# First unit of a latent projection: products ordered by high and low parts, input scales on ScalarE's DMA queue, the sum of squares half a unit later

## The chip, the cores and the metric

The kernel runs on one core of a Trainium2 chip. The metric is the device time of one execution in microseconds; the time before is the median of three runs. Engines are named as the profile names them: PE is TensorE, DVE is VectorE, ACT is ScalarE, POOL is GpSimd, SP is SyncE. DMAs are issued here from SP and, in a few places, from ACT.

## The reference

Two transformer-like blocks run one after the other on 512 tokens of width 1024. Only the beginning of the first matters for this change:

```
u = x * rsqrt(mean(x*x) + EPS) * g_mix_pre
z = u @ w_in[0]
... q_lat, kv_lat, k_rope are columns of z ...
q = rmsnorm(q_lat) * g_q_lat @ w_q_up
k_pe = rope(k_rope, positions)
```

Behind it follow latent attention, a gated convolution, a mixing layer, a feed-forward layer, gated linear attention and an indexed sparse attention. They are computed as before.

## The kernel before, in words

All matrices are kept in f32 and every product is made of three matmuls on rounded parts. A weight block `w` becomes `w_hi` (rounded) and `w_lo` (what is left), an operand becomes `op_hi` and `op_lo`; `split_mm` (lines 747 to 753) issues hi x hi, hi x low operand and low weight x hi into one PSUM bank. The sequence on every engine is written out by hand, and engines meet at counting semaphores. `Steps` names each step of a stage (`hi3`, `lo3`, `acc7`, `sum`), and `at("acc7")` is the count to wait for.

Weights come in **units** of 512 KB, eight blocks of 128 x 128. SP loads a unit into one of four `raw` buffers. POOL splits it: line 723 writes `w_hi` and raises `hi_ready`, line 725 writes `w_lo` and raises `split_ready`. There are two split slots, so POOL may begin unit u only when PE has finished unit u-2 (`unit_done`).

The first four units, 0 to 3, hold w_in for four output tiles, two of the eight contraction blocks k in each (`blockwise`): unit 0 has k = 0 and 1, unit 1 has 2 and 3, unit 2 has 4 and 5, unit 3 has 6 and 7. Banks 0 to 3 take all of them, so each unit is 24 matmuls. Units 4 and 5 hold one further output tile each.

In stage `start` the input x arrives transposed in `h`, in eight tiles of 128 x 512. For each tile m:

- ACT (line 1683) writes `op_hi[m]` = rounded h[m] times its gain column, step `hi{m}`; it then squares h[m] (line 1686), step `sq{m}`;
- DVE writes `op_lo[m]` (line 2408), step `lo{m}`, and adds the square to a running sum (line 2405), step `acc{m}`.

The gain columns (`gain`, 289 per partition) arrive by one DMA. The norm of x is not applied to the operand; the sum of squares is taken over partitions by one matmul with ones, `full_sum(4)` (line 769), step `sum`. ACT takes the root (line 1649), DVE the reciprocal (`rs`, line 2484), and the projected tiles are multiplied by `rs` when they leave PSUM (`z0`, `z1`, ...: line 2402). Between `rs` and `z0` DVE's list also holds the rotary angles, in this order: `pos` (line 2487), `ang0` (2451), `turn` (2454), `whole` (2456), `red1` to `red3` (2408), `clip` (2461). Then come `z0`, `z1`, `z2`, and `acc1`, `acc2`, the sum of squares of the query latent. PE, in stage `lat`, does six of the eight blocks of unit 4 (18 matmuls), waits for `acc2`, does `sum_q` (line 775), the last two blocks, `root_q` (line 789), and goes on to unit 5. That is the only way into the rest of the program.

PE's order before is units 0 and 1, then `sum`, then units 2 and 3.

Of the kernel before, what the change touches and what calls it, by code (L numbers as in the profile page):

```python
# [50 lines left out]
U0 = {}  # L51
# [156 lines left out]
def build(nc, ins, out):  # L208
    ctx = ExitStack()
    with ctx:  # L210
# [7 lines left out]
        w_hi = sb("w_hi", [P, SLOTS, 8, P], F32R)  # L218
        w_lo = sb("w_lo", [P, SLOTS, 8, P], F32R)
        op_hi = sb("op_hi", [P, KD, T], F32R)  # L220
        op_lo = sb("op_lo", [P, KD, T], F32R)
# [10 lines left out]
        gain = sb("gain", [P, GAINS], F32)  # L232
        st = sb("st", [P, 64], F32)
        ps = [ctx.enter_context(nc.psum_tensor(f"bank{b}", [P, T], F32)) for b in range(8)]
# [109 lines left out]
        hi_ready = sem("hi_ready")  # L344
        half_hi, half_ready = sem("half_hi"), sem("half_ready")
        split_ready = sem("split_ready")
        unit_done = sem("unit_done")
        gain_in, p_in, pos_in = sem("gain_in"), sem("p_in"), sem("pos_in")
        x_in = [sem(f"x_in{n}") for n in range(KD // 2)]
        x_first = sem("x_first")  # L350
        cst_in, out_sem = sem("cst_in"), sem("out_sem")
# [206 lines left out]
        def enter(eng, who, name, others=("act", "dve", "pe"), after=None, drained=True):  # L558


            k = ORDER.index(name)
            if k:
                before = S[after or ORDER[k - 1]][who]
                eng.wait_ge(before.sem, before.total)
            if who == "pe":
                used = U0[name] if name in U0 else 0
                if used and drained:
                    eng.wait_ge(unit_done, used)
            mine = S[name][who]
            eng.sem_inc(mine.sem, mine.credit)  # L570
            for other in others:
                if other != who:
                    eng.wait_ge(S[name][other].sem, S[name][other].credit)
            return S[name]["act"], S[name]["dve"], S[name]["pe"]
# [5 lines left out]
        def _(sp):  # L580
# [37 lines left out]
            n = LOADS  # L618
            load_from(0, 0)
            sp.dma_start(h[:, 0], ins["x"][0]).then_inc(x_first, 16)  # L620
            sp.dma_start(gain[:, :], ins["gains"]).then_inc(gain_in, 16)
            sp.dma_start(h[:, 1], ins["x"][1]).then_inc(x_in[0], 16)
            load_from(1, 1)
            for k in range(1, KD // 2):
# [123 lines left out]
        def _(pe):  # L748
# [18 lines left out]
            def full_sum(bank, x=acc):  # L767

                return pe.matmul(ps[bank][:, :], ones, x, start=True, stop=True)
# [22 lines left out]
            def blockwise(u0, before, units=range(4)):  # L792

                d = S[before]["dve"]
                for c in units:
                    pe.wait_ge(split_ready, u0 + c + 1)
                    for kk in range(2):
                        k = 2 * c + kk
                        pe.wait_ge(d.sem, d.at(f"lo{k}"))
                        for m in range(4):  # L800
                            mm = split_mm(ps[m][:, :], w_hi[:, (u0 + c) % 2, 4 * kk + m], w_lo[:, (u0 + c) % 2, 4 * kk + m],
                                          op_hi[:, k], op_lo[:, k], k == 0, k == KD - 1)
                    mm.then_inc(unit_done, 1)

            a, d, z = enter(pe, "pe", "start")
            blockwise(U0["lat"], "start", range(2))
            pe.wait_ge(cst_in, 16)
            pe.wait_ge(d.sem, d.at("acc7"))
            z.done(full_sum(4), "sum")
            blockwise(U0["lat"], "start", range(2, 4))  # L810

            a, d, z = enter(pe, "pe", "lat", ())
            u = U0["lat"]
# [17 lines left out]
            a, d, z = enter(pe, "pe", "attn", ())  # L831
# [88 lines left out]
            for k in range(2):  # L920
                u = attn_unit(f"V{k}")
                pe.wait_ge(split_ready, u + 1)
                wh, wl = [w[:, u % 2, 0:4].rearrange("p k n -> p (k n)") for w in (w_hi, w_lo)]
                for t in range(QT):
                    mm = split_mm(ps[3 + t][:, :], kvn_hi[:, k, t * P:(t + 1) * P], kvn_lo[:, k, t * P:(t + 1) * P], wh, wl, k == 0, k == 1)
                mm.then_inc(unit_done, 1)
            for p in range(NH // 2):
                x, y = 2 * p, 2 * p + 1
# [41 lines left out]
            a, d, z = enter(pe, "pe", "mix", ())  # L970
# [17 lines left out]
            u = U0["mix"]  # L988
# [12 lines left out]
            a, d, z = enter(pe, "pe", "wo", ())  # L1001
            for m in range(KD):
                u = U0["wo"] + m
# [22 lines left out]
            a, d, z = enter(pe, "pe", "res1", (), drained=False)  # L1026
# [13 lines left out]
            u = U0["up0"]  # L1040
            for c in range(4):
                s = (u + c) % 2
                pe.wait_ge(split_ready, u + c + 1)
                for kk in range(2):
                    k = 2 * c + kk
# [7 lines left out]
                    for m in range(4):  # L1053
                        mm = pe.matmul(ps[m][:, :], w_hi[:, s, 4 * kk + m], op_lo[:, k], start=False, stop=k == KD - 1)
# [6 lines left out]
            for n, x in enumerate((acc, fx[:, 11, :])):  # L1061
# [4 lines left out]
                for t in range(QT):  # L1066
                    mm = pe.matmul(ps[5][:, t:t + 1], x[:, t * P:(t + 1) * P], ones[:, 0:1], start=n == 0 and t == 0, stop=n == 1,
                                   skip_group_check=True)
# [6 lines left out]
            for half in (0, 1):  # L1075
                name = f"up{half}"
                a, d, z = enter(pe, "pe", name, () if half == 0 else ("act", "dve", "pe"))
                u = U0[name]
# [24 lines left out]
                a, d, z = enter(pe, "pe", name, ())  # L1103
                if half == 0:
                    with pe.Fori(0, 2) as i:
                        for m2 in range(2):
# [3 lines left out]
                            for v in range(3):  # L1110
                                c = 3 * m2 + v
                                pe.wait_ge(split_ready, i * 6 + (U0[name] + c + 1))
                                for kb in range(8):
# [3 lines left out]
                                    m, k = n // HJ, n % HJ  # L1117
# [8 lines left out]
                else:  # L1126
                    for g in range(KD // 2):
# [3 lines left out]
                        for v in range(3):  # L1131
                            u = U0[name] + 3 * g + v
                            pe.wait_ge(split_ready, u + 1)
                            for kb in range(min(8, 2 * HJ - 8 * v)):
                                m, k = divmod(8 * v + kb, HJ)
# [507 lines left out]
        def _(act):  # L1643
# [23 lines left out]
            def proj_out(name, m, bank):  # L1667
# [5 lines left out]
                    act.wait_ge(unit_done, U0[name] + 1)  # L1673
                hi(a, f"e{m}", ebuf[:, m, :], ps[bank][:, :])

            act.wait_ge(cleared, 1)
            act.activation(st[:, 62:63], st[:, 63:64], ACT.Sqrt, bias=st[:, 63:64])
            act.wait_ge(gain_in, 16)
# [1913 lines left out]
```

## Time and profile before

| | |
|---|---|
| time, median of 3 runs | 1747.75 us (1746.61 to 1748.42) |
| the profiled execution's own time | 1746.92 us |
| its span, first to last instruction | 1745.1 us |
| mean granted TensorE clock | 0.996 |
| PE busy | 98% of the span |
| DVE, ACT, POOL busy | 59%, 36%, 57% |

The span lies inside the execution's own time, 1.8 us of which are outside it. The chain that ended last is 87% PE over the whole program; the busy share of PE says little of the first 60 us, in which other engines feed it, and those are what the change touches. Times in the text are microseconds from the span's start unless a whole time is meant.

### The profile page before, as it was taken

Reading aid. Unit: us, or ns where it says so; the run is one execution under the profiler, and the core shown is the slowest. Engines: PE = TensorE matmul, PEld = TensorE weight load, DVE = VectorE, ACT = ScalarE, POOL = GpSimd, SP = SyncE. Lnnn points to the kernel's source line nnn. Section 1 sums busy time; section 2 is a strip of 40 time slices with the busy share of each in tenths; the row PEclk is TensorE's granted clock in tenths of the full one; section 3 lists DMA queues with packets and bytes.
Section 4 is the critical chain, followed back from the end, with each engine's and each line's share of the span. In section 5 each row is a group of like instructions: output and inputs, shape, how many; then the busy total and the mean of one; then the engine's idle time right before and its main releaser. Section 6 shows DMA issues by size and latency. Waiting matters only on the chain.

```text
span 1745.1 us, 22351 instructions
## 1 busy us (share of the span) xinstructions
PE 1709.6 (98%) x7966; PEld 1418.3 (81%) x7966; DVE 1023.3 (59%) x1680; ACT 629.4 (36%) x1182; POOL 986.5 (57%) x586
## 2 busy tenths in 40 slices
PE   7999999999999999998999999999999999999998
PEld 6788788788877888887788888888878888888887
DVE  6778543345651554254778745646757977776244
ACT  4455311243312222043734332332433127766022
POOL 5655466666666666664664556555565663333654
PEclk9999999999999999998999999999999999999999
DMA  5222222222223222322222222222232221111222
GB/s 205 91 76 86 81 97 96 97 94 88 97 97 109 90 98 93 105 97 85 90 80 73 85 73 92 77 85 72 85 103 85 85 97 61 49 49 61 85 86 83
DMA packets 49768, 154.36 MB, mean 88 GB/s; under 512 B 8976, under 2 KB 9104, under 8 KB 49552
## 3 DMA queue, kind: packets, MB, share of 16 engines
q1 hardware_dynamic: 48816, 151.59, 26.1%
q10 hardware_dynamic: 864, 1.57, 0.3%
q8 instruction: 58, 0.95, 0.2%
q14 instruction: 30, 0.25, 0.0%
HBM read 151.05 MB, written 2.10 MB: 88 GB/s over the span
## 4 chain that ended last, share of the span: by engine, by line
PE 87%; DVE 6%; ACT 3%; issue 3%; DMA 0%; POOL 0%; SPq 0%; DVEq 0%; ACTq 0%; POOLq 0%
PE bank L751 26%; PE bank L753 25%; PE bank L752 25%; DVE r L2399 1%; PE bank L1547 1%; PE bank L1153 1%; PE bank L1154 1%; PE bank L1157 1%; ACT r L1645 1%; PE bank L1386 1%; PE bank L1390 1%; PE bank L1387 1%; DVE fx L2402 1%; DVE bank L2405 1%; PE bank L900 1%
## 5 line engine op out<-in xcount | busy, mean ns | idle before, releaser
L723 POOL TENSOR_SCALAR w_hi<-raw 128x1024 fp32r<-128x1024 f32 (+1 forms) x279 | 296.6, 1063 | 682.4 <-issue 498.0
L725 POOL TENSOR_TENSOR w_lo<-raw,w_hi 128x1024 fp32r<-128x1024 f32 (+1 forms) x279 | 665.5, 2385 | 23.3
L751 PE MATMUL bank<-op_hi,w_hi 128*128 128x512 f32 x984 | 392.0, 398 | 13.9 <-DVE op_lo L2408 9.3
L753 PE MATMUL bank<-op_hi,w_lo 128*128 128x512 f32 x984 | 385.0, 391 | 0.0
L752 PE MATMUL bank<-op_lo,w_hi 128*128 128x512 f32 x984 | 384.7, 391 | 0.0
L751 PE MATMUL bank<-r,w_hi 128*128 128x512 f32 x856 | 339.8, 397 | 3.6 <-POOL w_lo L725 1.4
L753 PE MATMUL bank<-r,w_lo 128*128 128x512 f32 x856 | 333.9, 390 | 0.0
L752 PE MATMUL bank<-r,w_hi 128*128 128x512 f32 x856 | 333.7, 390 | 0.0
L751 PEld LDWEIGHTS bank<-op_hi,w_hi 128*128 128x128 f32 x984 | 186.1, 189 | 53.7 <-ACT bank L1686 9.3
L753 PEld LDWEIGHTS bank<-op_hi,w_lo 128*128 128x128 f32 x984 | 185.5, 189 | 39.4
L752 PEld LDWEIGHTS bank<-op_lo,w_hi 128*128 128x128 f32 x984 | 186.1, 189 | 37.2 <-issue 1.0
L751 PEld LDWEIGHTS bank<-r,w_hi 128*128 128x128 f32 x856 | 160.8, 188 | 38.6 <-issue 3.5
L753 PEld LDWEIGHTS bank<-r,w_lo 128*128 128x128 f32 x856 | 160.7, 188 | 34.1
L752 PEld LDWEIGHTS bank<-r,w_hi 128*128 128x128 f32 x856 | 161.0, 188 | 29.9
L1645 ACT ACTIVATE r<-bank 128x512 fp32r<-128x512 f32 (+6 forms) x173 | 85.2, 508 | 162.0 <-DVE bank L2402 84.9
L2399 DVE TENSOR_TENSOR r<-bank,r 128x512 fp32r<-128x512 f32 (+6 forms) x172 | 95.3, 574 | 62.3 <-ACT r L1645 61.2
L2399 DVE TENSOR_TENSOR r<-fx,r 128x512 fp32r<-128x512 f32 (+3 forms) x64 | 75.3, 1176 | 61.1 <-ACT r L1645 60.7
L1645 ACT ACTIVATE r<-fx 128x512 fp32r<-128x512 f32 (+3 forms) x64 | 46.5, 726 | 161.7 <-DVE fx L2405 71.9
L2408 DVE SCALAR_TENSOR_TENSOR fx<-bank,gain,fx 128x511 f32<-128x511 f32 x88 | 65.9, 749 | 46.8 <-ACT fx L1898 43.0
L2405 DVE TENSOR_TENSOR eb<-eb,bank 128x512 f32<-128x512 f32 x48 | 32.6, 684 | 96.4 <-PE bank L753 96.1
L2402 DVE TENSOR_TENSOR bank<-bank,fx 128x512 f32<-128x512 f32 x78 | 54.2, 696 | 54.8 <-PE bank L753 49.1
L752 PE MATMUL bank<-r 128*128 128x128 f32 (+7 forms) x256 | 80.5, 314 | 0.0
(277 smaller groups left out, 2432.7 us busy)
## 6 DMA issues: line engine op xcount, KB each, us to landing
raw<-in_weights SPq DMA_DIRECT2D x276, 512.0 KB, 3.3
out<-h SPq DMA_DIRECT2D x8, 256.0 KB, 2.0
h<-in_x SPq DMA_DIRECT2D x3, 512.0 KB, 9.0
cst<-in_consts SPq DMA_DIRECT2D x1, 1156.5 KB, 12.1
rope_cos<-in_p ACTq DMA_DIRECT2D x3, 256.0 KB, 3.6
rope_sin<-in_p ACTq DMA_DIRECT2D x3, 256.0 KB, 3.9
h<-in_x SPq DMA_DIRECT2D x2, 256.0 KB, 5.0
rope_cos<-in_positions SPq DMA_DIRECT2D x2, 256.0 KB, 12.0
```

The source lines that it names most:

```text
L723: pool.tensor_scalar(hi, raw[:, r, at:w], 1.0, 0.0, ALU.mult, ALU.add).then_inc(hi_ready, 1)
L725: pool.tensor_tensor(lo, raw[:, r, at:w], hi.bitcast(F32), ALU.subtract).then_inc(split_ready, 1)
L751: pe.matmul(o, ah, bh, start=start, stop=False, skip_group_check=skip)
L752: pe.matmul(o, ah, bl, start=False, stop=False, skip_group_check=skip)
L753: return pe.matmul(o, al, bh, start=False, stop=stop, skip_group_check=skip)
L900: mm = pe.transpose(ps[5 + q % 2][:, kt * P:(kt + 1) * P], p[:, kt * P:(kt + 1) * P], ident)
L1153: pe.matmul(ps[m][:, :], w_hi[:, s, 4 * kk + m], op_hi[:, k], start=k == 0, stop=False)
L1645: steps.done(act.activation(o, i_, ACT.Copy), name)
L2399: steps.done(dve.tensor_tensor(o, src, high.bitcast(F32), ALU.subtract), name)
L2402: steps.done(dve.tensor_tensor(o, x, y, ALU.mult), name)
L2405: steps.done(dve.tensor_tensor(o, x, y, ALU.add), name)
L2408: steps.done(dve.scalar_tensor_tensor(out=o, in0=x, scalar=s, in1=y, op0=op0, op1=op1), name)
```

## The change

Three things, all in the first 60 us:

1. The load of the gain columns is issued by ACT as its first instruction, no longer by SP as its third.
2. Unit 0 is computed in another order: the eight hi x hi products of k = 0 and 1 first, waiting for `hi_ready`, `hi0` and `hi1`; then the eight with `w_lo`, waiting for `split_ready`; then the eight with `op_lo`, waiting for `lo0` and `lo1`. PE no longer waits at its start for ACT and DVE to have entered the stage.
3. `sum` is issued behind k = 4, the fifth block, that is in the middle of unit 2, no longer between units 1 and 2.

```diff
-            sp.dma_start(gain[:, :], ins["gains"]).then_inc(gain_in, 16)
...
-            a, d, z = enter(pe, "pe", "start")
-            blockwise(U0["lat"], "start", range(2))
-            pe.wait_ge(cst_in, 16)
-            pe.wait_ge(d.sem, d.at("acc7"))
-            z.done(full_sum(4), "sum")
-            blockwise(U0["lat"], "start", range(2, 4))
+            a, d, z = enter(pe, "pe", "start", ())
+
+            def first_terms(u, k, w, x, start=False, stop=False):
+                for m in range(4):
+                    mm = pe.matmul(ps[m][:, :], w[:, u % 2, 4 * (k % 2) + m], x[:, k], start=start, stop=stop)
+                return mm
+
+            u = U0["lat"]
+            pe.wait_ge(hi_ready, u + 1)
+            for k in range(2):
+                pe.wait_ge(a.sem, a.at(f"hi{k}"))
+                first_terms(u, k, w_hi, op_hi, start=k == 0)
+            pe.wait_ge(split_ready, u + 1)
+            for k in range(2):
+                first_terms(u, k, w_lo, op_hi)
+            for k in range(2):
+                pe.wait_ge(d.sem, d.at(f"lo{k}"))
+                mm = first_terms(u, k, w_hi, op_lo)
+            mm.then_inc(unit_done, 1)
+            blockwise(u, "start", range(1, 2))
+            pe.wait_ge(split_ready, u + 3)
+            for k in (4, 5):
+                pe.wait_ge(d.sem, d.at(f"lo{k}"))
+                for m in range(4):
+                    mm = split_mm(ps[m][:, :], w_hi[:, u % 2, 4 * (k % 2) + m], w_lo[:, u % 2, 4 * (k % 2) + m], op_hi[:, k], op_lo[:, k], False, False)
+                if k == 4:
+                    pe.wait_ge(cst_in, 16)
+                    pe.wait_ge(d.sem, d.at("acc7"))
+                    z.done(full_sum(4), "sum")
+            mm.then_inc(unit_done, 1)
+            blockwise(u, "start", range(3, 4))
...
+            act.dma_start(gain[:, :], ins["gains"]).then_inc(gain_in, 16)
             act.wait_ge(cleared, 1)
```

The instruction lists show the two moves on PE. At its start, PE before, the first rows of unit 0 (a line number is one of the kernel's, `waits` names the semaphores):

```order
L751 MATMUL bank0<-op_hi,w_hi 128x512 [waits split_ready,dve_start,act_start]
L752 MATMUL bank0<-op_lo,w_hi 128x512
L753 MATMUL bank0<-op_hi,w_lo 128x512
L751 MATMUL bank1<-op_hi,w_hi 128x512
L752 MATMUL bank1<-op_lo,w_hi 128x512
```

The same place in the changed kernel:

```order
L808 MATMUL bank0<-op_hi,w_hi 128x512 [waits act_start,hi_ready]
L808 MATMUL bank1<-op_hi,w_hi 128x512
L808 MATMUL bank2<-op_hi,w_hi 128x512
L808 MATMUL bank3<-op_hi,w_hi 128x512
L808 MATMUL bank0<-op_hi,w_hi 128x512 [waits act_start]
L808 MATMUL bank1<-op_hi,w_hi 128x512
L808 MATMUL bank2<-op_hi,w_hi 128x512
L808 MATMUL bank3<-op_hi,w_hi 128x512
L808 MATMUL bank0<-op_hi,w_lo 128x512 [waits split_ready]
```

The first eight products need neither low part any more. On PE between unit 1 and unit 2 stood, before:

```order
L751 MATMUL bank3<-op_hi,w_hi 128x512
L752 MATMUL bank3<-op_lo,w_hi 128x512
L753 MATMUL bank3<-op_hi,w_lo 128x512
L769 MATMUL bank4<-fx,cst 128x512 [waits dve_start,cst_in]
L751 MATMUL bank0<-op_hi,w_hi 128x512 [waits dve_start,split_ready]
L752 MATMUL bank0<-op_lo,w_hi 128x512
```

There now (lines of the changed file are one lower here):

```order
L750 MATMUL bank3<-op_hi,w_hi 128x512
L751 MATMUL bank3<-op_lo,w_hi 128x512
L752 MATMUL bank3<-op_hi,w_lo 128x512
L750 MATMUL bank0<-op_hi,w_hi 128x512 [waits dve_start,split_ready]
L751 MATMUL bank0<-op_lo,w_hi 128x512
L752 MATMUL bank0<-op_hi,w_lo 128x512
```

The sum has gone from this place; it stands twelve matmuls further on.

## Rows read from the trace of the kernel before

**Rows 1.** Chain that ended last, in order of time, 0 to 48 us: start, us, what
```profile
3.08 8.06 DMA h<-in_x
...
22.46 0.69 DVE fx L2405
...
23.29 1.11 PE bank L769 x2
...
39.76 1.05 PE bank L775 x8
```

**Rows 2.** Timeline of PE, 8.9 to 41 us: start, us, engine line op tiles
```profile
9.32 0.76 PE L751 MATMUL bank<-op_hi,w_hi 128*128 128x512 f32 x1 [9.32 <-DVE op_lo L2408]
...
14.57 0.46 PE L751 MATMUL bank<-op_hi,w_hi 128*128 128x512 f32 x1
14.88 0.40 PE L752 MATMUL bank<-op_lo,w_hi 128*128 128x512 f32 x1
...
23.82 0.79 PE L751 MATMUL bank<-op_hi,w_hi 128*128 128x512 f32 x1
24.45 0.40 PE L752 MATMUL bank<-op_lo,w_hi 128*128 128x512 f32 x1
...
29.48 0.39 PE L753 MATMUL bank<-op_hi,w_lo 128*128 128x512 f32 x1
...
34.92 0.39 PE L753 MATMUL bank<-op_hi,w_lo 128*128 128x512 f32 x1
...
39.00 0.39 PE L753 MATMUL bank<-op_hi,w_lo 128*128 128x512 f32 x1
```

**Rows 3.** Timeline of POOL, 8 to 66 us
```profile
18.15 1.05 POOL L723 TENSOR_SCALAR w_hi<-raw 128x1024 fp32r<-128x1024 f32 x1 [4.57 <-DMA raw<-in_weights]
19.29 2.71 POOL L725 TENSOR_TENSOR w_lo<-raw,w_hi 128x1024 fp32r<-128x1024 f32 x1
...
30.06 1.13 POOL L723 TENSOR_SCALAR w_hi<-raw 128x1024 fp32r<-128x1024 f32 x1 [3.32 <-issue]
31.27 2.71 POOL L725 TENSOR_TENSOR w_lo<-raw,w_hi 128x1024 fp32r<-128x1024 f32 x1
35.50 1.14 POOL L723 TENSOR_SCALAR w_hi<-raw 128x1024 fp32r<-128x1024 f32 x1 [1.52 <-issue]
```

**Rows 4.** Chain that ended last, DVE's part from the cast to the clip
```profile
28.47 0.37 DVE fx L2487
...
30.32 1.42 DVE fx L2408
...
31.76 2.78 DVE fx L2408
...
34.56 0.70 DVE fx L2408
...
35.29 0.44 DVE fx L2461
```

**Rows 5.** One line's instructions over the whole span: duration ns min/median/max
```profile
L2469 DVE TENSOR_SCALAR rope_sin<-rope_sin,cst x3: 480/1276/2608, 40.5 to 531.6; 128x512 f32<-128x512 f32 x3
```

**Rows 6.** DMA issues over the whole span: KB each, median us from issue to landing
```profile
rope_cos<-in_p ACTq DMA_DIRECT2D x3, 256.0 KB, 3.6
...
h<-in_x SPq DMA_DIRECT2D x2, 256.0 KB, 5.0
...
gain<-in_gains SPq DMA_DIRECT2D x1, 144.5 KB, 5.7
```

**Rows 7.** Windows around another idle stretch of PE: busy PE, PEld, DVE, ACT, POOL; PEclk; DMA
```profile
796.00:799.00 3.00, 2.08 (x12) 2.00 (x11) 0.18 (x1) 1.04 (x3) 0.95 (x1) 0.56 0.27 75
799.00:802.00 3.00, 0.70 (x3) 0.43 (x3) 2.50 (x4) 0.60 (x1) 0.00 (x0) 0.50 0.25 100
802.00:805.00 3.00, 3.00 (x8) 2.32 (x8) 2.89 (x6) 1.78 (x3) 0.00 (x0) 0.50 0.00 0
```

**Rows 8.** A window of 5 us at the start: the last three columns are PEclk, DMA share, GB/s
```profile
15.00:20.00 5.00, 5.00 (x24) 4.10 (x23) 5.00 (x8) 4.14 (x7) 1.77 (x2) 1.00 1.03 406
```

## The prediction

> **What bounds the kernel now.** I read the page's chain first: 87% PE. Then the chain in order of time for the first 48 us, because the change touches nothing else, and there it is not PE that leads [rows 1]. The last input tiles' DMA (till 11.14) leads to ACT and DVE, the last addition of squares ends at 23.15, `sum` runs at 23.29, then one ACT instruction for the root, and from there DVE (and ACT once more) until `sum_q` at 39.76. PE works meanwhile, but `sum_q` starts 0.76 after the 18th matmul of unit 4 (39.00) [rows 2], where one matmul follows another in 0.23: it waits for DVE. So up to 39.76 PE's start does not set the end; the moment of `sum` and what delays DVE after it do.
>
> What delays DVE is POOL. `red1`, `red2` and `red3` are the same operation, and take 1.42, 2.78 and 0.70 [rows 4]. POOL's two splits of unit 4 run from 30.06 to 31.19 and from 31.27 to 33.98 [rows 3]: red1 ends 0.55 behind the first, red2 0.56 behind the second, and the second split itself, begun under red1, takes 2.71. One waits for the other to finish. Against 0.70 to 0.74 undisturbed, DVE loses 0.7 + 2.0 = 2.7 here. A TENSOR_SCALAR suffers as well: 480 ns at best, 2608 at worst [rows 5]. Instructions with a PSUM input (`z0`, `acc2`) are spared: the timeline has 0.68 to 0.70 for each.
>
> The Trainium skill says the same in "SBUF — State Buffer", Who interferes with whom: the shared port pair is held for a whole instruction and the loser blocks. By that rule, the trace agrees.
>
> **The early start.** A DMA issued by ACT has no row at this place; the nearest are ACT's loads of `p`, landed 3.6 after issue, and the same gain load on SP's queue, issued at 1.67 and 5.7 under way [rows 6]. Issued at about 0.75, gain lands between 4.4 and 6.5 instead of 7.4, the bounds of an unknown that turns out not to matter. The first four products can start at about 6; the next four need tile 1, landed at 8.5 before (issued at 2.14; the two single tiles took 3.6 and 6.4, median 5.0 [rows 6]), so `hi1` ends near 9.2. PE's first twelve matmuls take 9.32 to 14.57, 0.43 each but the first (1.2 GHz), and from there one takes 0.23 (2.4 GHz): 5.25 after it began [rows 2]. Twenty matmuls from 9.3 on end at 14.7 if the first four count towards that, at 16.4 if not. Unit 1, 24 x 0.2275 = 5.5, ends at 20.2 to 21.9; before it was 22.9. That is a gain of 1 to 2.7 on PE, but POOL has unit 2's low parts only at 19.29 + 2.71 = 22.00 [rows 3], and before them POOL waited 4.57 for that unit's transfer [rows 3]. So **unit 2 starts at T = 22.05**, not 23.82 [rows 2].
>
> **The sum.** It now stands behind twelve matmuls of unit 2: 0.31 for the first (as 14.57 to 14.88, behind a change of pace) and 11 x 0.2275 = 2.8, so it runs at 24.86 instead of 23.29: **1.57 later**. `acc7` (23.15) no longer makes it wait. For PE the sum costs 0.53 itself and 0.63 until the second matmul behind it, which is 0.93 more than a normal step. Root, reciprocal and everything on DVE until the cast follow at before's distance of 5.18 (23.29 to 28.47 [rows 1, 4]), so the cast asks at 30.04.
>
> **Where POOL is then.** The last matmul of unit 2 starts 5.66 after its first (23.82 to 29.48 [rows 2]); without the 0.63 in front (-0.32) and with the sum inside (+0.93) that is 22.05 + 6.27 = 28.32, and POOL begins unit 4 0.58 later as before (29.48 to 30.06 [rows 2, 3]): high parts 28.90 to 29.95, low parts 30.04 to 32.40. That meets the cast in the same hundredth. Whoever comes first, DVE loses the 2.4: either the cast or the next TENSOR_SCALAR waits to 32.4. Then pos ends at 32.6, red1 starts 1.49 later (28.83 to 30.32) at 34.1 and runs to 34.84. PE's last matmul of unit 3 is 5.44 behind that of unit 2 (34.92 - 29.48), 33.76, and POOL asks for unit 5 at 34.34. It gets the ports behind red1, till 35.8; red2 ends at 36.35; the low parts, asked for at 35.9, run 36.25 to 38.6; red3 ends at 39.15. The clip starts at 39.2 instead of 35.29. Before, unit 5's split began at 35.50, just behind red3 [rows 3, 4]; now both splits of two units fall into the angle chain. DVE loses 2.2 + 0.75 + 2.0 = 5.0 instead of 2.7.
>
> From clip to `sum_q` there were 4.47 (35.29 to 39.76 [rows 1, 4]), PSUM operations and ACT: `sum_q` at 43.6, **3.8 later** (1.57 + 2.3).
>
> **What it costs PE.** PE reaches that place at 22.05 + 15.18 - 0.32 + 0.93 = 37.84 for the 18th matmul (15.18 is 39.00 - 23.82 [rows 2]), and could do `sum_q` at 38.1. It stands for 5.5. After an idle stretch the granted clock falls: around 796 to 805 PE was idle in pieces, and PEclk reads 0.56, then 0.50 [rows 7]. Estimate for here, from the 5.25 at the start and those 0.50 windows: about five microseconds from `sum_q` on at the lower level, some 7 to 12 full matmuls at 0.43 instead of 0.23 and the small ones between them, 1.4 to 2.4. Short waits of PE on other engines behind it can swallow a little. I take **1.6**; ends 0 (no fall) and 2.4.
>
> The issue on ACT costs nothing: ACT had only its table load to do until gain landed at 7.4. SP's later issues come 0.47 sooner, but the DMA share is full, 1.03, from 15 to 20 [rows 8]; I give nothing, and up to 0.5. All else behind 60 us keeps its distances.
>
> Sum: +3.8 + 1.6 = +5.4, on the profiled execution 1746.92 -> 1752.3. The median shown is 0.8 above that execution; I state **1753.0** against 1747.75. What a measurement here tells from no change is 0.2%, 3.5 us.
>
> **Rivals.**
>
> *A, forecast:* 1751.3 to 1755.3, chance 0.66. For it: the whole lead is on DVE and every distance is taken from rows.
>
> *B, the sum is late but the locks are kind.* If POOL's unit 5 finds DVE past red3, or the cast and its followers slip through, DVE loses the same 2.7 as before, `sum_q` comes 1.57 later, PE stands 3.2 and the clock may stay: +1.6 to +3.4, about 1750.0. Against it: DVE would have to be over two microseconds ahead of the distances worked out. Chance 0.20.
>
> *C, not slower: the transfers come sooner.* Tile 0 landed at 4.8 (1.20 + 3.6), gain at 7.4, so gain held the queue for 2.6, while tile 1 with 256 KB took 1.2 more. Laid beside the first transfers, gain could free up to 2.2 for all behind it. Unit 2's low parts then come at 19.8, T is set by PE at 20.2 to 21.9, and `sum` runs at 23.0 to 24.7. This decides only if T falls below 20.5, so that `sum` is no later than before, and DVE must be spared as in B: 1747.2, and at the very best 1745. Against: the DMA share is 1.03 [rows 8], and another order of the same bytes does not change that. Chance 0.09.
>
> The Trainium skill, "DMA: Bandwidth & Descriptors", Issuing engines are not separate DMA queues, says that issuing from several engines saves only the sequencer's issue time; by it C would have 0.47 (one SP issue), not 2.2. No run so far shows it for this place.
>
> *D, worse:* cold for longer, or another collision in stage `lat`: 1755.3 to 1758, chance 0.05. That gain on ACT's queue lands no sooner changes nothing above, since T hangs on POOL.
>
> **How the numbers follow.** The likeliest case gives 1753.0. The range leaves out most of C and D and a little of A: 1748.8 to 1755.3. Slower by over 0.2% is all of D and nearly all of A: 0.68. Faster by over 0.2% would need 3.5 us, more than all that PE starts sooner: 0.02. The rest, 0.30, is B and C.
>
> **What would show it.** PE's first matmul near 6 and a gap before the fifth; unit 2 at 22.0; line 768 near 24.9; DVE's cast or the next TENSOR_SCALAR at 2 to 2.7, two of the three line 2408 stretched; `sum_q` at 43 to 44 with PE idle over 4 before it; PEclk at 0.5 behind it. `sum_q` below 41.5 would prove the collisions wrong, a T below 21 the fixed transfers.

## The result, and the profile after

| | before | changed |
|---|---|---|
| median, 8 executions each, side by side | 1746.40 us (1744.99 to 1748.42) | 1751.53 us (1750.24 to 1752.44) |
| ratio, 95% interval | | 1.0031 [1.0022, 1.0039] |
| the profiled execution's own time | 1746.92 us | 1751.50 us |
| its span | 1745.1 us | 1749.7 us |
| mean granted TensorE clock | 0.996 | 0.993 |

The changed kernel is slower by 5.4 us by the ratio (0.0031 x 1746.4) and by 5.1 us by the two medians, in any case more than the 3.5 us that count as a difference. A second measurement of it, with a trace of its own, gave 1.0031 [1.0019, 1.0043] against 1745.85. Three executions of later runs (2451.78 us of the kernel before, 1823.06 and 6104.7 us of a reordered one) lie far above the others of their kernel and are left out of every median and ratio given here.

The profile after, in the order of the rows before. The gain columns first: ACT's timeline (start, us, what, idle before and what ended it), and the row of the DMA issues.

```profile
0.75 0.42 ACTq L1700 DMA_DIRECT2D gain<-in_gains  x1
...
5.41 0.72 ACT L1708 ACTIVATE op_hi<-h,gain 128x512 fp32r<-128x512 f32 x1 [2.62 <-DMA h<-in_x]
```

```profile
gain<-in_gains ACTq DMA_DIRECT2D x1, 144.5 KB, 4.0
```

Gain is there 4.0 after its issue, and the first high part ends at 6.1. (In the trace of before it took 5.7 [rows 6], but in a second trace of the kernel before, told of below, 4.1: that much of the difference is not the change's.) PE's timeline, same columns:

```profile
6.28 3.40 PE L808 MATMUL bank<-op_hi,w_hi 128*128 128x512 f32 x8 [6.28 <-ACT op_hi L1708]
9.52 1.98 PE L808 MATMUL bank<-op_hi,w_lo 128*128 128x512 f32 x8
11.34 1.98 PE L808 MATMUL bank<-op_lo,w_hi 128*128 128x512 f32 x8
...
20.69 0.50 PE L750 MATMUL bank<-op_hi,w_hi 128*128 128x512 f32 x1 [1.64 <-POOL w_lo L724]
...
23.56 1.02 PE L768 MATMUL bank<-fx,cst 128*128 128x512 f32 x2
...
36.48 0.39 PE L752 MATMUL bank<-op_hi,w_lo 128*128 128x512 f32 x1
41.94 1.87 PE L774 MATMUL bank<-cst,fx 128*128 128x1 f32 x8 [5.08 <-DVE fx L2430]
43.67 0.77 PE L750 MATMUL bank<-op_hi,w_hi 128*128 128x512 f32 x1
44.24 0.63 PE L751 MATMUL bank<-op_lo,w_hi 128*128 128x512 f32 x1
...
47.33 0.47 PE L750 MATMUL bank<-op_hi,w_hi 128*128 128x512 f32 x1
```

PE starts 3 us sooner than in the trace of before (9.32 [rows 2]; 2.4 sooner than in the second one, 8.70). It stands 1.64 ahead of unit 2 because the low weights are not there, and 5.08 ahead of `sum_q`, which comes at 41.94 and not at 39.76 [rows 1]. Behind that idle stretch the six full matmuls between `sum_q` and `root_q` follow one another in 0.43; the full pace is back at 47.33. Before, a wait of 0.37 left the clock as it was; here the granted clock falls. The windows show it (busy PE, PEld, DVE, ACT, POOL; then PEclk, DMA share, GB/s):

```profile
40.00:45.00 5.00, 3.06 (x11) 2.87 (x12) 2.91 (x7) 3.32 (x6) 0.00 (x0) 0.50 0.00 2
45.00:50.00 5.00, 5.00 (x24) 4.14 (x24) 3.08 (x5) 1.83 (x3) 3.07 (x4) 0.83 0.00 0
```

POOL's timeline, the splits of units 2 (low parts), 4 and 5:

```profile
17.96 2.67 POOL L724 TENSOR_TENSOR w_lo<-raw,w_hi 128x1024 fp32r<-128x1024 f32 x1
...
27.53 1.05 POOL L722 TENSOR_SCALAR w_hi<-raw 128x1024 fp32r<-128x1024 f32 x1 [2.98 <-issue]
28.66 2.61 POOL L724 TENSOR_TENSOR w_lo<-raw,w_hi 128x1024 fp32r<-128x1024 f32 x1
32.97 1.14 POOL L722 TENSOR_SCALAR w_hi<-raw 128x1024 fp32r<-128x1024 f32 x1 [1.70 <-issue]
34.20 2.70 POOL L724 TENSOR_TENSOR w_lo<-raw,w_hi 128x1024 fp32r<-128x1024 f32 x1
```

and the chain of waits, DVE's part from the cast to the clip (start, us, what):

```profile
28.66 0.37 DVE fx L2512
29.06 2.51 DVE fx L2476
...
32.52 0.70 DVE fx L2433
33.24 1.42 DVE fx L2433
34.68 2.77 DVE fx L2433
37.48 0.44 DVE fx L2486
```

Unit 4's high parts fall under the reciprocal and hold nobody, but each of the next three splits stretches an instruction, where two were stretched before [rows 4]. `ang0` (2.51 for 0.49) ends 0.30 behind unit 4's low parts; `red2` (1.42 for 0.70) ends 0.55 behind unit 5's high parts, and `red3` (2.77) 0.55 behind its low parts. DVE loses 2.0 + 0.7 + 2.05 = 4.8, against 2.7 before. The cast itself slipped through: it ran 28.66 to 29.03, beside the low parts' first moments.

How much the slow matmuls cost can be read up to the first matmul at full pace, the one behind `root_q`'s eight. In PE's timeline of before it was this:

```profile
42.95 0.47 PE L751 MATMUL bank<-op_hi,w_hi 128*128 128x512 f32 x1
```

From `sum_q` to it are 3.19 before (42.95 - 39.76) and 5.39 after (47.33 - 41.94): 2.20 for the clock. With the 2.18 by which `sum_q` is late that is 4.38 of the 4.58 between the two profiled executions (1751.50 - 1746.92). That so little is left over is partly luck: what lies behind that matmul took 1702.2 and 1702.4 in these two executions, but 1701.5 to 1704.5 over all fourteen traces.

### The profile page after: what moved, and what is told of

The parts are those of the page before. It is cut to its first block, busy times and chain, and to the rows that moved or that the text cites. A ratio compares the mean times of both kernels' runs of the same rounds, so it can differ in the third digit from the quotient of the medians.

```text
span 1749.7 us, 22350 instructions
## 1 busy us (share of the span) xinstructions
PE 1711.7 (98%) x7966; PEld 1419.6 (81%) x7966; DVE 1027.2 (59%) x1680; ACT 629.4 (36%) x1182; POOL 986.3 (56%) x586
## 4 chain that ended last, share of the span: by engine, by line
PE 88%; DVE 6%; ACT 3%; issue 2%; POOL 0%; DMA 0%; DVEq 0%; SPq 0%; ACTq 0%; POOLq 0%
PE bank L750 26%; PE bank L752 26%; PE bank L751 26%; DVE r L2424 1%; PE bank L1571 1%; PE bank L1177 1%; PE bank L1178 1%; PE bank L1181 1%; ACT r L1669 1%; PE bank L1410 1%; DVE fx L2427 1%; PE bank L1411 1%; PE bank L1414 1%; PE bank L774 1%; PE bank L924 1%
```

## The experiments

The last two runs are told first, because they change how the two traces above are compared.

### The kernel before once more, and the changed kernel once more

No edit. The profile of before that the prediction used is one execution, and `sum` stood there at 23.29, hardly sooner than the 23.56 of the changed kernel, where the forecast had 1.57 between them.

> The kernel before itself, for its trace on another chip. In the runs with the gain load still on SP, x and the weights landed 1 to 2 us sooner than in the first trace of this kernel, so that acc7 ended at 19.7 and 21.2 and not at 23.15. If that is chance or the chip and not the edit, this trace shows an acc7 between 19.5 and 22 too, the sum behind unit 1 at 22.1 to 22.4, and sum_q near 38.6 instead of 39.76.

It was executed once, in 1747.17 us. Its timeline of PE, `sum` and `sum_q`:

```profile
21.81 1.10 PE L769 MATMUL bank<-fx,cst 128*128 128x512 f32 x2
...
38.29 1.05 PE L775 MATMUL bank<-cst,fx 128*128 128x1 f32 x8 [0.38 <-DVE fx L2405]
```

> The changed kernel itself, beside the kernel before on the same chip and in the same stretch of time as the two others. 5.1 to 5.5 us over the kernel before, sum_q near 41.5, PEclk at 0.5 behind it.

1751.54 us, 1.0031 [1.0019, 1.0043]; `sum` at 23.68, `sum_q` at 42.08 behind 5.09 idle, as in the first trace (0.6 later than expected). The first full-pace matmul comes at 48.05 here: 5.97 behind `sum_q`, so the clock cost 2.78 in this execution.

The kernel before, run again, starts everything some 1.5 us sooner than in its first trace. The first trace was late, and a comparison with it alone hides most of the delay of `sum`. With the traces of the other experiments a table can be made that takes the scatter of the first transfers out. The reference point is the end of POOL's low parts of unit 2:

| trace | low parts end | `sum` behind them | `sum_q` behind `sum` | PE idle before `sum_q` |
|---|---|---|---|---|
| before | 22.00 | 1.29 | 16.47 | 0.37 |
| before, again | 20.51 | 1.30 | 16.48 | 0.38 |
| before + gain on ACT | 21.04 | 1.30 | 16.48 | 0.40 |
| new order of unit 0 alone | 20.04 | 1.29 | 16.49 | 0.40 |
| before + `sum` behind k = 4 | 21.31 | 3.70 | 18.40 | 5.09 |
| changed | 20.63 | 2.93 | 18.38 | 5.08 |
| changed, again | 20.77 | 2.91 | 18.40 | 5.09 |

The scatter is in the first column, and the third and fourth do not share it. `sum` is 2.93 - 1.29 = 1.64 later in the changed kernel, and from there to `sum_q` it takes 18.38 - 16.47 = 1.91 longer.

### Each part alone

The `sum` put back between units 1 and 2 in the changed kernel:

```diff
             blockwise(u, "start", range(1, 2))
+            pe.wait_ge(cst_in, 16)
+            pe.wait_ge(d.sem, d.at("acc7"))
+            z.done(full_sum(4), "sum")
             pe.wait_ge(split_ready, u + 3)
...
-                if k == 4:
-                    pe.wait_ge(cst_in, 16)
-                    pe.wait_ge(d.sem, d.at("acc7"))
-                    z.done(full_sum(4), "sum")
```

> The changed kernel with only the sum put back between units 1 and 2. DVE theory (what counts is when the sum lets DVE begin, and which of POOL's splits DVE then meets): acc7 ends at 21.8 in the changed kernel, so the sum runs at 21.9 instead of 23.56; PE stands from 18.9 to 21.9; from there every distance is that of the kernel before, 1.4 us sooner, with DVE losing 2.7 to POOL and not 4.8; sum_q near 38.4, no fall of the clock; 1745.0 against 1746.4 before. PE theory (what counts is that PE does not stand idle at its start): PE idles 3 us more than in the changed kernel and the time is 1752 or more.

1746.42 us, 1.0002 [0.9993, 1.0011]. The loss is gone, but the 1.4 us of gain that were expected are missing. The profiled execution (1746.96) shows one way in which they are lost: PE now stands still ahead of `sum`. PE's timeline, then DVE's and POOL's:

```profile
23.13 1.10 PE L768 MATMUL bank<-fx,cst 128*128 128x512 f32 x2 [3.48 <-DVE fx L2429]
...
24.38 0.63 PE L751 MATMUL bank<-op_lo,w_hi 128*128 128x512 f32 x1
...
27.36 0.50 PE L752 MATMUL bank<-op_hi,w_lo 128*128 128x512 f32 x1
```

```profile
18.67 2.27 DVE L2432 SCALAR_TENSOR_TENSOR op_lo<-h,gain,op_hi 128x512 fp32r<-128x512 f32 x1
...
21.46 0.92 DVE L2432 SCALAR_TENSOR_TENSOR op_lo<-h,gain,op_hi 128x512 fp32r<-128x512 f32 x1
22.30 0.68 DVE L2429 TENSOR_TENSOR fx<-bank,fx 128x512 f32<-128x512 f32 x1
```

```profile
17.69 2.71 POOL L724 TENSOR_TENSOR w_lo<-raw,w_hi 128x1024 fp32r<-128x1024 f32 x1
20.35 1.49 POOL L722 TENSOR_SCALAR w_hi<-raw 128x1024 fp32r<-128x1024 f32 x1
```

PE is through with unit 1 sooner, so POOL may go on from unit 2 to unit 3 without a pause (20.35; before it began at 23.20 and, in the second trace, at 22.11). That split (20.35 to 21.84) holds `lo7`, after the low parts had held `lo6`, and `acc7` ends at 22.98. PE had finished early, idled 3.48, and then one matmul followed another in 0.43 from 24.38 to 27.36. In this execution the port and then the clock took back what the early start gave. Whether all executions went that way I can't say from one trace.

The gain columns alone, in the kernel before:

```diff
             sp.dma_start(h[:, 0], ins["x"][0]).then_inc(x_first, 16)
-            sp.dma_start(gain[:, :], ins["gains"]).then_inc(gain_in, 16)
             sp.dma_start(h[:, 1], ins["x"][1]).then_inc(x_in[0], 16)
...
+            act.dma_start(gain[:, :], ins["gains"]).then_inc(gain_in, 16)
             act.wait_ge(cleared, 1)
```

> The kernel before with only the gain load issued by ACT. Transfer theory: tile pairs and weights land as in the changed kernel (tiles 2 and 3 at 9.3 instead of 11.1, unit 2's weights at 16.5 instead of 18.1), acc7 ends near 21.8, the sum runs at 21.9, sum_q at 38.4: -1.4 us, about 1745.0, the same as with the new order of unit 0. Rival (only one issue slot of 0.47 us on SP is saved, and the rest of the earlier landing came from elsewhere): sum at 22.8, 1745.9.

1746.57 us, 1.0003 [0.9994, 1.0012]: nothing, and the expectation of -1.4 us was wrong. PE's first matmul was at 9.32. That is no sooner than in the first trace of before and later than in its second (8.70). PE waits for the first low parts of the operand, and DVE began these at 6.57 (8.42 and 6.89 in the two traces of before). But POOL's low parts of unit 0 ran from 6.28 to 8.63 beside them, and the first two instructions took 4.05 together, where they took 3.19 in the second trace of before and 0.75 each in the first. POOL was late here because unit 0's weights landed later: it began unit 0 at 5.15, in the two traces of before at 4.49 and 4.52. So this edit is not without effect, only without effect on the time. The Trainium skill, "DMA: Bandwidth & Descriptors", Issuing engines are not separate DMA queues, holds that another issuing engine saves only the time of the issue; this run agrees with it.

The new order of unit 0 alone (the changed kernel with gain back on SP's queue, where it was, and `sum` back as in the diff above):

> Only the new order of unit 0; gain on SP's queue and the sum where they were. DVE theory: hi0 begins at 7.55 as before, PE's first product at 8.3 instead of 9.3, unit 1 ends 1 to 1.5 us sooner, and then PE waits longer for acc7 at 23.15; sum and all behind it as before, 1746.4 within 0.3. PE theory: 1 us faster, 1745.4.

1745.51 us, 0.9997 [0.9988, 1.0006]. PE starts at 6.83, 1.9 sooner than in the second trace of before, and the time does not move, as expected. DVE is further ahead here than with `sum` put back and gain on ACT: the low parts of unit 2 hold `lo7` itself (18.31 to 20.59), not `lo6`. So when POOL began unit 3 at 20.84 nothing was left that it could hold, and `acc7`, with one input in PSUM, ended at 21.19.

`sum` alone, in the kernel before:

```diff
-            pe.wait_ge(cst_in, 16)
-            pe.wait_ge(d.sem, d.at("acc7"))
-            z.done(full_sum(4), "sum")
-            blockwise(U0["lat"], "start", range(2, 4))
+            u = U0["lat"]
+            pe.wait_ge(split_ready, u + 3)
+            for k in (4, 5):
...
+                if k == 4:
+                    pe.wait_ge(cst_in, 16)
+                    pe.wait_ge(d.sem, d.at("acc7"))
+                    z.done(full_sum(4), "sum")
```

> The kernel before with only the sum moved behind k = 4. DVE theory: the sum runs at 25.6 instead of 23.29 (+2.3), POOL's split of unit 4 at 29.6 to 33.1 meets cast and scalings, that of unit 5 meets red2 and red3, DVE loses 4.8 instead of 2.7, sum_q at 44.1 (+4.3), PE idle over 5 us before it, granted clock at 0.5 behind it for another 2.2: 1752.9, +6.5. Rival (the position of the sum costs only its own delay): +2.3, 1748.7, and no fall of the clock.

1752.82 us, 1.0036 [1.0023, 1.0050]: 6.3 us slower by the ratio, where 6.5 were expected. PE's timeline:

```profile
25.01 1.02 PE L769 MATMUL bank<-fx,cst 128*128 128x512 f32 x2
...
43.41 1.87 PE L775 MATMUL bank<-cst,fx 128*128 128x1 f32 x8 [5.09 <-DVE fx L2413]
```

So the place of `sum` is the whole of the loss, and the other two edits give nothing by themselves. Together with it they give a little: with PE's old order unit 2 starts only at 22.29, 0.98 after its low weights, and `sum` stands 3.70 behind these instead of 2.93. The changed kernel measures 1.0031 and this one 1.0036, but the two intervals overlap.

### The cold clock taken away

If the clock costs 2.2 us, a PE that does not stand still should give that back while `sum_q` stays late. In the changed kernel PE got 21 matmuls without use, into a bank that is free at this time, ahead of its wait for `acc2`:

```diff
             blocks(ps[5][:, :], 0, [(k, k) for k in range(6)], op_hi, op_lo, stop=False)
+            for n in range(21):
+                pe.matmul(ps[6][:, :], w_hi[:, 0, n % 6], op_hi[:, n % 6], start=True, stop=True)
             pe.wait_ge(d.sem, d.at("acc2"))
```

> The changed kernel with 21 extra matmuls (4.8 us, into bank 6, whose contents unit 5 overwrites) in front of PE's wait for acc2; they only fill its idle time. Clock theory: sum_q starts at 41.9 as in the changed kernel, but the granted clock stays at 1.00 and the eight groups behind it run at 0.23 a matmul: 2.2 us less than the changed kernel, about 1749. Rival (the clock falls for another reason, or the slow stretch is hidden by waits): no change, 1751.

1749.18 us, 1.0017 [1.0008, 1.0026], against 1745.80 beside it. PE's timeline and a window of this kernel:

```profile
41.33 1.05 PE L774 MATMUL bank<-cst,fx 128*128 128x1 f32 x8 [0.35 <-DVE fx L2432]
```

```profile
40.00:45.00 5.00, 4.65 (x29) 3.83 (x28) 3.55 (x8) 2.97 (x6) 0.83 (x2) 1.00 0.00 2
```

From `sum` to `sum_q` are 18.41 as in the changed kernel, and PEclk stays at 1.00. The first matmul behind `root_q` comes 3.21 after `sum_q`, not 5.39: 2.18 come back in the trace. In the time it is 2.4 us by the ratios (1.0031 - 1.0017) and 1.8 by the medians, each against the kernel before beside it (5.13 and 3.38 above it). That is the price of the fall, shown by taking away the idle stretch alone. What is left, 0.0017 x 1745.8 = 3.0, is the late `sum_q`, for which the table has 1.64 + 1.91 = 3.5.

### The port taken away from part of DVE's chain

The three `red` read two tiles of SBUF each. With the tile of turns in PSUM they read one:

```diff
-            angles(d, fx[:, 9:10, :], fx[:, 10:11, :], fx[:, 10, :], [0])
+            angles(d, fx[:, 9:10, :], ps[6][:, :].rearrange("p (a t) -> p a t", a=1), fx[:, 10, :], [0])
```

> The changed kernel with the tile of turns, one of the two inputs of red1 to red3, in PSUM instead of SBUF; POOL works as before. Port theory (an instruction of DVE with two SBUF inputs waits for POOL's split): turn and whole take 0.25 longer each, red2 and red3 lose nothing, 0.7 each instead of 1.42 and 2.77, clip at 35.2 instead of 37.48, sum_q at 39.6: 2.3 us less, and up to 2.2 more if PE's idle time, 2.8 instead of 5.1, is too short for the clock to fall: 1746.5 to 1748.7. Rival (red2 and red3 are long for another reason, such as the order of their waits): they stay at 1.4 and 2.8, 1751.

1750.30 us, 1.0023 [1.0014, 1.0032], above the 1746.5 to 1748.7 that were expected. DVE's timeline, and POOL's beside it:

```profile
29.25 2.50 DVE L2476 TENSOR_SCALAR fx<-fx,cst 128x512 f32<-128x512 f32 x1
...
32.50 0.70 DVE L2481 TENSOR_SCALAR bank<-bank 128x512 f32<-128x512 f32 x1
33.24 2.14 DVE L2433 SCALAR_TENSOR_TENSOR fx<-bank,fx 128x512 f32<-128x512 f32 x3
35.41 1.56 DVE L2486 TENSOR_SCALAR fx<-fx 128x512 f32<-128x512 f32 x1
```

```profile
33.16 1.06 POOL L722 TENSOR_SCALAR w_hi<-raw 128x1024 fp32r<-128x1024 f32 x1 [1.70 <-issue]
34.30 2.39 POOL L724 TENSOR_TENSOR w_lo<-raw,w_hi 128x1024 fp32r<-128x1024 f32 x1
```

The port theory holds for the three `red`: they take 2.14 together, 0.71 each, while both of POOL's splits run over them, and POOL's take 1.06 and 2.39 where they took 1.14 and 2.70. But the size was off. The clip, with its tile in SBUF, now meets the same low parts and takes 1.56 for 0.43, and the two instructions that write PSUM take 0.69 and 0.70 instead of 0.43. Of the 2.8 saved on `red1` to `red3`, 1.7 go out again; `sum_q` is 17.27 behind `sum` instead of 18.38. The clock still falls, against the hope of the expectation: PE idles 3.96 and PEclk reads 0.71 from 40 to 45.

### Angles ahead of the reciprocal

The angles need nothing from `sum`. DVE stands idle for 3.61 between `acc7` and the root; could it do them there?

```diff
-              + ["rs", "pos", "ang0", "turn", "whole", "red1", "red2", "red3", "clip"],
+              + ["pos", "ang0", "turn", "whole", "red1", "red2", "red3", "clip", "rs"],
```

In the code the reciprocal and its wait go behind the call of `angles` accordingly. Once in the changed kernel:

> The changed kernel with DVE's list reordered: pos, the angles and the clip right behind acc7, the reciprocal rs behind them. Nothing on PE moves. DVE theory: the 7 us of angles, with what POOL takes of them, now run beside units 2 and 3 while ACT and PE make the sum, rs ends at 32 to 33, where PE ends unit 3, z0 to acc2 follow, and sum_q starts at 36.8 to 37.5 instead of 41.94 with PE idle under 1 us and no fall of the granted clock: 6 to 7 us less than the changed kernel, about 1744 against 1745.5 before. Rival (the later sum as such, or PE's own order, costs the time): rs cannot begin before the sum, so the time stays within 1 us of the changed kernel's 1751.

and once in the kernel before:

> The same reordering of DVE alone on the kernel before. DVE theory: there PE waited only 0.4 to 0.8 us at sum_q, so the reordering can give back no more than that: 1744.7 to 1745.1. If it gives 2 us or more, PE's early idle time at the sum was not what it ran into.

1745.41 us (1743.83 to 1748.99), 0.9995 [0.9986, 1.0004], and 1745.18 us, 0.9997 [0.9988, 1.0006]. The 5.4 us of the changed kernel are gone, so DVE's chain was their only way into the time. But neither clearly beats the kernel before, and the first missed its expectation of 1744. Its profiled execution was one of its two longest, 1748.92, and shows what made it so; DVE's timeline, then PE's:

```profile
22.48 2.00 DVE L2510 CAST fx<-rope_cos 128x512 f32<-128x512 int32 x1
...
28.86 2.51 DVE L2486 TENSOR_SCALAR fx<-fx 128x512 f32<-128x512 f32 x1
```

```profile
38.39 1.48 PE L774 MATMUL bank<-cst,fx 128*128 128x1 f32 x8 [2.24 <-DVE fx L2430]
```

The cast meets one of POOL's splits and the clip another, the reciprocal has to wait for both, and PE idles 2.24; PEclk reads 0.50 from 40 to 45. Whether the same was behind the other execution near 1749 I can't say, it has no trace; the nine others took 1743.83 to 1746.3.

### Reciprocal between the last `red` and the clip

The reciprocal reads one tile and took 3.34 or 3.35 in every trace, whatever POOL did. So it should stand where POOL's two splits of unit 4 fall, from about 27.9 to 31.8, behind everything that a split would hold:

```diff
-              + ["rs", "pos", "ang0", "turn", "whole", "red1", "red2", "red3", "clip"],
+              + ["pos", "ang0", "turn", "whole", "red1", "red2", "red3", "rs", "clip"],
...
                     sync(d, f"red{n + 1}")
+                between()
                 d.done(dve.tensor_scalar(ang, ang, PI, -PI, ALU.min, ALU.max), "clip")
```

`between` is the reciprocal with its wait for the root. In the changed kernel:

> The changed kernel with DVE's list in a third order: pos, ang0, turn, whole, red1 to red3 behind acc7, then the reciprocal rs, then the clip. With the angles first, the clip was held 2.1 us by POOL's split of unit 4 and only then rs could run, which has one input and waits for nobody. DVE theory: rs runs over that split, the clip ends at 32.7, z0 starts as soon as unit 3 is done, sum_q at 36.4 to 36.9 with PE idle under 1 us and the granted clock at 1.00 throughout: 2 us sooner at sum_q than the kernel before (38.8 in the run with the gain load on ACT), 1743.5 against 1745.7, and no executions near 1749 as with the angles first. Rival (early idle time of PE buys nothing in the end): 1745.5 as with the angles first.

and in the kernel before:

> The same third order of DVE's list on the kernel before, sum between units 1 and 2. PE reaches sum_q at 37.8 to 38.0 and cannot be sooner, as with the angles first on this kernel (38.04): 1745.2. The difference to the run before this one is what the new order of unit 0 and the later sum are worth once DVE does not wait: DVE theory 1 to 1.5 us in favour of the later sum. Rival (the later sum costs something in itself): no difference, or the old place is ahead.

In the changed kernel: 1743.75 us over ten executions (1743.04 to 1746.18), against 1745.85 of the kernel before beside it, 0.9988 [0.9979, 0.9997]. The median lies under those of both kernels, and the interval lies below 1, if by little. With the PE order of the kernel before it is 1745.18 us, 0.9998 [0.9989, 1.0007]. The first one's timelines of DVE, POOL and PE:

```profile
28.45 3.35 DVE L2511 RECIPROCAL fx<-fx 128x512 f32<-128x512 f32 x1
31.72 0.37 DVE L2487 TENSOR_SCALAR fx<-fx 128x512 f32<-128x512 f32 x1
33.30 1.89 DVE L2427 TENSOR_TENSOR fx<-bank,fx 128x512 f32<-128x512 f32 x3 [1.20 <-PE bank L752]
```

```profile
27.94 1.40 POOL L722 TENSOR_SCALAR w_hi<-raw 128x1024 fp32r<-128x1024 f32 x1 [2.91 <-issue]
29.42 2.39 POOL L724 TENSOR_TENSOR w_lo<-raw,w_hi 128x1024 fp32r<-128x1024 f32 x1
```

```profile
37.11 0.95 PE L774 MATMUL bank<-cst,fx 128*128 128x1 f32 x8
```

The reciprocal runs over the low parts' split and neither is held (the high parts' 1.40 instead of 1.05 is a wait for the last `red`), DVE is ready 1.20 before PE has the product for `z0`, and `sum_q` starts without a wait. Now PE's own start decides, and there the changed kernel's order is worth something: `sum_q` at 37.11 against 37.66, and measured from the end of unit 2's low parts 16.05 against 17.23. By the medians it is 1.4 us, and eight of the ten executions lie below all eleven of the other; the intervals of the two ratios overlap, so that this difference is likely but not settled. At 0.12% the whole gain over the kernel before is itself below the 0.2% named in the prediction.

## Why the prediction was right, step by step

The forecast was 1753.0, case A, slower because `sum` is later, DVE collides more, and the clock falls. That is 5.25 above the median it was given, and 5.1 by the medians and 5.4 by the ratio were measured. The chain was right, from the late `sum` over DVE and POOL to PE's idle stretch and the clock. The sizes of its terms were not all as good as their sum, and what it says of the start was right only in its price.

**The early start is worth nothing (forecast 0).** Right. PE started at 6.28, stood 1.64 ahead of unit 2 for POOL's low parts, and the order alone measured 0.9997. The figure for the start of unit 2, 22.05, was wrong: it was 20.69, and the prediction had said that a value below 21 would prove the fixed transfers wrong. The transfers are not fixed, they scatter: `hi2`, which waits for its tile of x in every trace, began at 11.17 in the first trace of before and at 9.01 to 9.85 in the thirteen others. The six traces with the old order of unit 0 have the low parts' end at 20.43 to 22.00, the eight with the new one at 19.95 to 21.06. The trace on which 22.05 rests is the latest of all fourteen; I took one execution's landing times for the kernel's. Between the two middles, 20.9 and 20.5, lie some 0.4 that may be the change's own: in five of the six old traces POOL waited there for PE's unit 0, and only in the one that the forecast read for the transfer; in all of the new ones it waited for the transfer. So the forecast took the wrong wait for the usual one, and "worth nothing" is right to within that 0.4. The gap before the fifth product did not come either: tile 1 was there for a `hi1` that ended at 7.52, not 9.2, and the first eight products ran through in 3.40.

**`sum` 1.57 later.** Right as a distance: 1.64, measured from the low parts' end in both kernels. Against the one trace of before it looked like 0.27, since that one was 1.37 late. The row that should have warned is POOL's wait of 4.57 for the DMA [rows 3]: a place bound by a transfer scatters with it.

**Collisions, +2.3.** They were +1.91, nearly as put: three of the four splits of units 4 and 5 hold somebody in the angles, where before it was the two of unit 4. The walk through the hundredths named the cast or the next TENSOR_SCALAR, then `red2` and `red3`; it was the latter, `ang0`, and `red2` and `red3`. The reciprocal, which the forecast took at before's distance, was spared indeed. Moving one of the two inputs to PSUM set the three `red` free, so that for them the contention over SBUF inputs is shown and not only argued.

**PE idle for 5.5, clock +1.6.** The idle stretch was 5.08. The clock's cost was the term that was sized too small: 2.20 in the trace, 2.78 in the second trace of the changed kernel, 2.43 with `sum` moved alone (`sum_q` at 43.41, full pace at 49.03), all behind the same idle stretch of 5.1; 1.8 to 2.4 by the run with a busy PE. The forecast's own upper end was 2.4, twelve full matmuls at 0.2. In the first trace only six full matmuls ran slow (43.67 to 46.38, 1.2 more than before's six), but `sum_q` and its eight small matmuls lost 0.8 and `root_q`'s eight 0.15; and the waits behind it, which the forecast let swallow a little, swallowed nothing.

**The issue on ACT, nothing.** Right for the time (1.0003), but not because nothing moved. With gain issued first on ACT, POOL began unit 0 at 4.87 to 5.34 in eight traces; with gain on SP at 4.28 to 4.52 in six. So unit 0's weights landed later, POOL's splits of units 0 and 1 reached further into DVE's first two low parts, and these took 4.05 to 4.11 together in all eight, 2.93 to 3.19 in five of the six others. That is the opposite of what rival C hoped for, and C is out. Of rival B, the late `sum` with DVE spared, the runs show the half: its price for the sum, 1.6, is in the result, but nothing in the changed kernel spares DVE, and the clock, which it let stay after an idle stretch of 3.2, fell around one of 3.48.

Measured from the low parts on, the terms make 1.64 + 1.91 + 2.20 = 5.75. Less the 0.4 by which the low parts come sooner, if that is the change's, it is 5.35, which fits the 5.1 to 5.4 measured. On the pair of profiled executions it is 4.4 of 4.58 (5.75 less the 1.37 by which the low parts ended sooner), but two executions of the kernel before show how little one pair says: `sum_q` came 1.47 sooner in the second, which still took 0.25 longer. That the forecast came so near is partly luck: one term of the forecast that was 0.4 too high and one that was 0.6 too low made a sum that was better than its parts. The sign "`sum_q` at 43 to 44" failed with them (41.94); as a delay, `sum_q` came 3.55 later measured from the low parts (1.64 + 1.91), against 3.8 forecast.

## What to carry to other kernels

Before a reduction that feeds a second engine is moved back behind other work of PE, read what that engine does next: here 1.6 us of delay became more than 5, since DVE's list then met a helper's splits one unit further on, and the idle stretch of PE cost the clock behind it. Where two engines share a port, an order of the list can be found in which the instruction that is not held (one SBUF input, here the reciprocal) lies over the helper's work; that gave the one gain here (0.9988), where each of the three edits alone gave none. And a place that waits for a transfer is to be read from several executions, or as a distance from the transfer's landing.

## What the runs showed of the hardware that was not expected

- The clock fell around idle stretches of PE of 5.08, 3.96, 3.48 and even 2.24 us, but not after 1.64 or 0.40. It did not always fall within them: in the two traces of the changed kernel it did, some 2.1 and 0.9 before `sum_q`, but around 3.96, 3.48 and 2.24 PEclk still read 1.00 when PE began again and fell 0.4 to 1.1 later. It was back at 2.4 GHz by 47.33 in the changed kernel, 5.4 after `sum_q`'s start, and 4.6 after `sum`'s start (23.13 to 27.70) where 3.48 had gone before.
- In every one of the fourteen traces the last addition of squares began 0.45 to 0.48 behind the end of one of POOL's splits: in ten behind unit 2's low parts (21.10 behind 20.63 in the changed kernel), in three behind unit 3's high parts (22.30 behind 21.84 above), in one behind unit 2's high parts. `acc7` reads nothing that POOL writes; `lo7` ahead of it had waited for the port. So the end of the sum of squares hung on POOL in every one; what `sum` waited for was this in the old place, and the twelve matmuls behind unit 2's low parts in the new one.
- The integer cast, which reads one tile, is held as well: 2.00 for 0.36, as are TENSOR_SCALARs with one tile (2.50 for 0.49). The reciprocal, also with one tile, is not. The Trainium skill, "SBUF — State Buffer", Who interferes with whom, says that copies, casts and `tensor_scalar` can take the second port pair, and that other instructions with one SBUF input do not contend with GpSimd. The traces agree for the cast, the TENSOR_SCALARs and the reciprocal.
- The landing of the first transfers scatters: `hi2` began, behind its tile of x, at 11.17 and at 9.64 in two profiles of the same kernel before.
- A load issued first on ACT delayed one issued at the same time on SP: with the 144.5 KB of gain on ACT, POOL could begin on unit 0's weights at 4.87 to 5.34 in eight traces, without it at 4.28 to 4.52 in six, with no overlap between the two groups.
